# Scattering token rows from SBUF to expert slots, in a mixture-of-experts encoder layer

## The reference, cut to what matters

```
g_idx  = argmax of 4 group logits;  top-2 of the 8 experts in that group
w_pair = softmax(top_v) * g_w                     # two weights a token
dest   = slot of each (token, expert) pair, experts padded to blocks
xbuf   = x_pad[slot_tok]                          # rows by slot
out    = (silu(xb @ w_gate[e]) * (xb @ w_up[e])) @ w_down[e]
y      = sum over a token's two slots of w_pair * out
x      = LN(alpha * x + (1 + gate) * y)
```

## Time and profile before

| | |
|---|---|
| median of 3 runs | 1818.4 us (1818.11, 1818.4, 1822.61) |
| profiled execution | 1822.78 us |
| its span | 1820.8 us, mean granted clock 0.923 |
| PE busy | 1549.7 us (85%) |
| DVE, ACT, POOL busy | 610.3, 331.0, 112.4 us |
| moved by DMA | 298.91 MB |

### The profile page before, as it was taken

One profiled execution on the slowest core, in us unless ns is written; L12 is line 12 of the kernel. 1 busy time (PEld: TensorE's weight loads), 2 busy tenths in 40 slices (PEclk: granted clock), 3 DMA queues, 4 the chain that ended last, 5 costly groups with the idle time before them and its releaser, 6 DMA issues. The chain is left out here.

```text
span 1820.8 us, 21099 instructions
## 1 busy us (share of the span) xinstructions
PE 1549.7 (85%) x7448; PEld 864.4 (47%) x7449; DVE 610.3 (34%) x1045; ACT 331.0 (18%) x566; POOL 112.4 (6%) x110
## 2 busy tenths in 40 slices
PE   5999999868875889999899543899999999999948
PEld 1455544336761766666455341444444444444423
DVE  1222144536886333333576640111111111101007
ACT  1101122212223333333211100101010101011111
POOL 0000000000002000000000032111111111101100
PEclk7999999977896899999999756999999999999979
DMA  9101011050006020000311106988889889999937
GB/s 365 56 23 35 1 12 46 12 185 1 0 0 225 15 93 0 0 0 0 136 65 63 48 0 197 365 319 293 319 332 381 322 319 396 392 333 393 395 133 297
DMA packets 145973, 298.91 MB, mean 164 GB/s; under 512 B 25596, under 2 KB 35848, under 8 KB 144915
## 3 DMA queue, kind: packets, MB, share of 16 engines
q1 hardware_dynamic: 137412, 280.73, 42.0%
q0 software_dynamic: 8384, 16.81, 2.6%
q10 hardware_dynamic: 146, 0.98, 0.2%
HBM read 282.85 MB, written 25.73 MB: 169 GB/s over the span
## 5 line engine op out<-in xcount | busy, mean ns | idle before, releaser
L382 PE MATMUL ps<-w_in_tok,uT_tiles 128*128 128x512 f32 (+2 forms) x512 | 191.5, 535 | 1.2 <-ACT uT_tiles L303 1.2
L1799 PE MATMUL ps<-w_gate_sb,x_slotsT 128*128 x320 | 145.3, 608 | 9.9 <-issue 7.5
L1828 PE MATMUL ps<-w_down_sb,hidT 128*128 x320 | 142.1, 597 | 11.1 <-DVE hidT L1885 11.1
L1799 PE MATMUL ps<-w_up_sb,x_slotsT 128*128 x320 | 140.6, 592 | 0.0
L382 PEld LDWEIGHTS ps<-w_in_tok,uT_tiles 128*128 128x128 f32 x512 | 97.7, 192 | 89.8 <-issue 61.2
L1398 PE MATMUL ps<-w_out,hT 128*128 128x512 f32 x256 | 114.5, 601 | 0.0
L1880 DVE TENSOR_TENSOR hid<-silu_g,ps 128x512 f32<-128x512 f32 x20 | 13.8, 688 | 294.1 <-PE ps L1799 294.1
L463 PE MATMUL ps<-uT,mod 128*128 128x512 f32 x256 | 110.1, 592 | 1.7 <-ACTq L470 1.7
L1799 PEld LDWEIGHTS ps<-w_gate_sb,x_slotsT 128*128 128x128 f32 x320 | 60.2, 193 | 87.7 <-issue 87.7
L1799 PEld LDWEIGHTS ps<-w_up_sb,x_slotsT 128*128 128x128 f32 x320 | 60.8, 190 | 76.5 <-issue 76.5
L1828 PEld LDWEIGHTS ps<-w_down_sb,hidT 128*128 128x128 f32 x320 | 59.1, 190 | 79.7 <-issue 79.7
(11 more groups left out here) (372 smaller groups left out, 2026.8 us busy)
## 6 DMA issues: line engine op xcount, KB each, us to landing
light_gate_sb<-in_w_gate SPq DMA_DIRECT2D x20, 2048.0 KB, 13.2
light_up_sb<-in_w_up SPq DMA_DIRECT2D x20, 2048.0 KB, 19.4
light_down_sb<-in_w_down SPq DMA_DIRECT2D x20, 2048.0 KB, 13.6
w_gate_sb<-in_w_gate SPq DMA_DIRECT2D x12, 2048.0 KB, 9.8
w_up_sb<-in_w_up SPq DMA_DIRECT2D x12, 2048.0 KB, 15.2
w_down_sb<-in_w_down SPq DMA_DIRECT2D x12, 2048.0 KB, 20.1
uT<-in_w_ada SPq DMA_DIRECT2D x8, 2048.0 KB, 9.9
y_pair<-expert_rows SPq DMA_DIRECT2D x8, 1024.0 KB, 10.7
```

The source lines that it names most:

```text
L382: mm = nc.tensor.matmul(ps[:, 2 + g, 0:n], uTt[:, j, k, :], wt[:, k, c0:c0 + n], start=k == 0, stop=k == KD - 1)
L1799: m = m_.matmul(ps[:, bank, :], xT[:, k, :], wt[:, bass.ds(buf, 1), k, :].rearrange("p a f -> p (a f)"), start=k == 0, stop=k == KD - 1)
L1828: m = m_.matmul(ps[:, 5 + half, :], hT[:, k, :], wd[:, bass.ds(buf, 1), k, half * 512:half * 512 + 512].rearrange("p a f -> p (a f)"), sta ...
```

## The change

The u2 rows now stay in SBUF. A tensor `big` (128 x 8 x 1024) lives for the whole kernel and is in turn uT, the keys and values of attention, u2, and the light gate and up weights.

- mLSTM stage: POOL zeroes `gate2`, and SP writes it over all 7680 slot rows of a DRAM tensor `xslots` in six DMAs; the stage ends when they have landed.
- Attention stage: behind `w_out`, SP copies `xslots` to `yslots` from DRAM to DRAM in six DMAs, awaited at the end of the output projection.
- Output projection: no store of u2; the router bias is loaded here.
- Routing: two products over all 256 columns give per-tile counts and ranks inside a tile; DVE sums the counts and adds them up tile by tile. The block table is made across 128 partitions, one block number a partition, and turned to one row by five small products. The pair weights are formed later. The map, its scatters and reads are gone.
- Experts: POOL first scatters the u2 rows to their slots (16 indirect DMAs of 128 rows), waits for all, and only then adds the increment that lets SP load light weights. A block's x is then a plain load of its slots, and y a plain store (five DMAs, the light block in four quarters).
- Combine: POOL gathers each tile's two y rows by slot.

```diff
@@ mlstm
+            def _(pool):
+                nc.gpsimd.memset(self.gate2[:], 0.0).then_inc(s_zero, 1)
...
+                n = NSLOT // P // 6
+                sp.wait_ge(s_zero, 1)
+                for i in range(6):
+                    sp.dma_start(rows[:, i * n:(i + 1) * n, :], self.gate2[:].unsqueeze(1).to_broadcast([P, n, D])).then_inc(s_cleared, 16)
+                sp.wait_ge(s_cleared, 16 * 6)
@@ attend
                 sp.dma_start(self.wo[:], self.i["w_out"].rearrange("(k p) n -> p k n", p=P)).then_inc(self.s_wo, 16)
+                n = NSLOT // 6
+                for i in range(6):
+                    sp.dma_start(self.yslots[i * n:(i + 1) * n, :], self.xslots[i * n:(i + 1) * n, :]).then_inc(self.s_yzero, 16)
@@ output_projection
+                sp.dma_start(self.br[:, 0:NG], self.i["b_rg"].partition_broadcast(P)).then_inc(s_br, 16)
+                sp.dma_start(self.br[:, NG:], self.i["b_re"].partition_broadcast(P)).then_inc(s_br, 16)
...
-                    sp.wait_ge(s_u, t + 1)
-                    sp.dma_start(u2_t[t], u2[:, t % 2, :]).then_inc(s_st[t % 2], 16)
+                sp.wait_ge(self.s_yzero, 16 * 6)
@@ routing
-                for t in range(TT):
-                    for j in range(t + 1):
-                        m = nc.tensor.matmul(ps[:, 0, t * E:(t + 1) * E], self.c(C_ONE if j < t else C_US), A[:, j, :], start=j == 0, stop=j == t)
-                for j in range(TT):
-                    m = nc.tensor.matmul(ps[:, 1, 0:E], self.c(C_ONE), A[:, j, :], start=j == 0, stop=j == TT - 1)
-                m.then_inc(s_rank, 1)
+                nc.tensor.matmul(ps[:, 1, 0:TT * E], self.c(C_ONE), Af, start=True, stop=True)
+                nc.tensor.matmul(ps[:, 0, 0:TT * E], self.c(C_US), Af, start=True, stop=True).then_inc(s_rank, 1)
+                pe.wait_ge(s_cols, 1)
+                for j in range(5):
+                    m = nc.tensor.matmul(ps[:, 2, j * NB:(j + 1) * NB], col[:, j:j + 1].to_broadcast([P, P]), self.c(C_ID, NB), start=True, stop=True)
+                m.then_inc(s_rows, 1)
...
+                lk(v.tensor_reduce(cnt[:], ps[:, 1, 0:TT * E].rearrange("p (t e) -> p e t", e=E), AX, ALU.add))
...
+                for t in range(TT - 1):
+                    lk(v.tensor_tensor(base[:, t + 1], base[:, t], ps[:, 1, t * E:(t + 1) * E], ALU.add))
...
+                lk(v.tensor_scalar(cmp_[:, 0], bend[:], pcol, None, ALU.is_le))
+                lk(v.tensor_scalar(cmp_[:, 1], lend[:], pcol, None, ALU.is_le))
...
+                lk(v.tensor_reduce(col[:], cmp_[:], AX, ALU.add))
+                v.tensor_scalar_min(col[:, 0:2], col[:, 0:2], float(E - 1)).then_inc(s_cols, 1)
...
+                for at, j in ((0, 0), (6, 1), (1, 2), (3, 3), (2, 4)):
+                    lk(v.tensor_copy(self.tbl[:, at], row(j)))
@@ experts
+                def load(b):
+                    g.dma_start(xg[:], self.xslots[b * P:(b + 1) * P, :]).then_inc(s_xg, 16)
...
+                def store(b):
                     pool.wait_ge(s_yd, b + 2)
+                    g.dma_start(self.yslots[b * P:(b + 1) * P, :], ys[:]).then_inc(s_out, 16)
                     pool.wait_ge(s_lyd, b + 2)
+                    rows = self.yslots[LB + b * LC:LB + (b + 1) * LC, :]
+                    for q in range(4):
+                        g.dma_start(rows[:, q * Q:(q + 1) * Q], yl[q * LC:(q + 1) * LC, :]).then_inc(s_lout, 16)
...
+                for k in range(2):
+                    for t in range(TT):
+                        g.indirect_dma_start(out=self.xslots, out_offset=bass.IndirectOffsetOnAxis(ap=self.posi[:, k, t:t + 1], axis=0),
+                                             in_=self.big[:, t, :], in_offset=None).then_inc(s_x0, 16)
+                pool.wait_ge(s_x0, 16 * 2 * TT)
+                pool.sem_inc(s_lG, 1)
+                load(0)
+                load_light(0)
@@ combine
+            def _(pool):
+                for t in range(TT):
+                    if t >= B:
+                        pool.wait_ge(s_sum, t - B + 1)
+                    for k in range(2):
+                        nc.gpsimd.indirect_dma_start(out=yt[:, t % B, k, :], out_offset=None, in_=self.yslots,
+                                                     in_offset=bass.IndirectOffsetOnAxis(ap=self.posi[:, k, t:t + 1], axis=0)).then_inc(s_y[t % B], 16)
```

More of the change, by code:

```diff
@@ L45 @@
 C_IOTA = C_INV + 32
-C_END = C_IOTA + NB
+C_PCOL = C_IOTA + NB
+C_END = C_PCOL + 1
 def constants():
@@ L67, in constants @@
     c[:, C_IOTA:C_IOTA + NB] = np.arange(NB)
+    c[:, C_PCOL] = np.arange(P)
     return c
@@ L732, in mlstm, with _ @@
             chunk = lambda i, d: i if d == 0 else i * -1 + (TT - 1)
+            @block.gpsimd
+            def _(pool):
+                nc.gpsimd.memset(self.gate2[:], 0.0).then_inc(s_zero, 1)
+            @block.sync
+            def _(sp):
+                rows = self.xslots.rearrange("(r p) d -> p r d", p=P)
+                n = NSLOT // P // 6
[3 more added lines that the diff above has]
+                sp.wait_ge(s_cleared, 16 * 6)
             @block.scalar
@@ L1282, in output_projection @@
             "varA", "stdA", "varB", "stdB", "u2_ready", "u2_turned", "u2T_ready", "logits_product", "logits_copied"))
-        s_st = [self.sem(f"u2_stored{j}") for j in range(2)]
+        s_br = self.sem("b_router_loaded")
         s_x1, s_x1st = self.sem("x1_ready"), self.sem("x1_stored")
@@ L1315, in _ @@
                     sp.dma_start(x1_t[t], x1[:, t, :]).then_inc(s_x1st, 16)
-                    sp.wait_ge(s_u, t + 1)
-                    sp.dma_start(u2_t[t], u2[:, t % 2, :]).then_inc(s_st[t % 2], 16)
-                for j in range(2):
-                    sp.wait_ge(s_st[j], 16 * TT // 2)
+                sp.wait_ge(s_br, 32)
+                sp.wait_ge(self.s_yzero, 16 * 6)
                 sp.wait_ge(s_x1st, 16 * TT)
@@ L1511, in routing @@
             hv, lt, lend = sb("is_heavy", [P, E]), sb("is_light", [P, E]), sb("light_end", [P, E])
[L1512 removed]
+            hst, prev = sb("heavy_start", [P, E]), sb("start_ahead", [P, E + 1])
+            base = sb("slot_base", [P, TT, E])
             pos = sb("pos", [P, 2, TT])
[L1514 to L1544 removed]
+            cmp_ = sb("cmp", [P, 5, E])
+            col = sb("table_cols", [P, 5])
             @block.scalar
@@ L1646, in _ @@
[L1646 to L1653 removed]
+                lk(v.tensor_copy(self.posi[:], pos[:]))
@@ new lines, in _ @@
+                dve.wait_ge(s_e2, 1)
+                lk(v.tensor_scalar_add(sel[:], eg[:], 1.0))
+                lk(v.reciprocal(sel[:], sel[:]))
+                lk(v.tensor_tensor(self.wts[:, 0], sel[:], gw[:], ALU.mult))
+                lk(v.tensor_tensor(self.wts[:, 1], eg[:], self.wts[:, 0], ALU.mult))
+                dve.wait_ge(s_rows, 1)
+                row = lambda j: ps[0:1, 2, j * NB:(j + 1) * NB]
+                for at, j in ((0, 0), (6, 1), (1, 2), (3, 3), (2, 4)):
+                    lk(v.tensor_copy(self.tbl[:, at], row(j)))
@@ L1656, in experts @@
+                lk(v.tensor_scalar_mul(self.tbl[:, 5], row(2), 16.0))
+                lk(v.tensor_tensor(self.tbl[:, 4, 0:1], bend[0:1, E - 1:E], lend[0:1, E - 1:E], ALU.max))
     def experts(self):
@@ L1757, in _ @@
                         pool.wait_ge(s_xt, b + 1)
-                        gather(ahead)
+                        load(ahead)
                         pool.wait_ge(s_lxt, b + 1)
-                        gather_light(ahead)
+                        load_light(ahead)
                     if b > 0:
                         with pool.If(n > b - 1):
-                            scatter(b - 1)
+                            store(b - 1)
             @block.tensor
@@ L1780, in _ @@
                 n = count(pe)
-                for s in (s_G, s_U, s_Y, s_ht, s_lG, s_lY, s_lht):
+                for s in (s_G, s_U, s_Y, s_ht, s_lY, s_lht):
                     pe.sem_inc(s, 1)
```

175 lines of the change are left out of this document (50 added, 125 removed).

## The result

The changed kernel took 1828.11 us (median of 13 runs, 1823.0 to 1835.2). The kernel before, run beside it, took 1822.15 us (13 runs, 1818.11 to 1826.91). The ratio is 1.0037, with a 95% interval of 1.002 to 1.0053: slower, by a little more than what can be told from no change. The forecast was 1802.0 with a range of 1786 to 1822. The profiled execution took 1830.28 us, its span 1828.4, at a mean granted clock of 0.923; the span is 7.6 us longer than before, where the forecast had 16.4 less.

The account below looks back on a forecast made before the run. Routing was taken as latency-bound, the experts as PE with DMA right behind, the combine as PE. Terms -15.2 - 6.7 + 3 + 2 + 0.5 = -16.4 us on the 1818.4 median gave 1802.0 us, range 1786 to 1822.

Parts of the forecast that it names:

- start of routing: Routing's front: the earlier bias load saves 3.6 us, moving the exponential's wait and its two followers away saves 0.8 us.
- ranks: Routing: 44 small rank products become two with 256 columns, 19.1 us falling to 2.3, so -16.8 us.
- slots ready: Routing: the point at which DVE has the slots, forecast at 1053.8 against 1072.98 before.
- first scatter to the last landed: Before the experts: 16 POOL scatters share DMA bandwidth with heavy weights, starting at 1061.6 and all landed by 1099.
- first x load: Before the first expert product: 4.7 us from issue to landing, plus 0.3, landed at 1104.0.
- first product: First expert product starts at 1108.1 instead of 1123.25, -15.2 us.
- first block: First expert block: light weights land before their use, removing the wait for light_up and the slow clock after it, -6.7 us.
- later blocks: Experts: whole blocks loaded and stored add DMA traffic, so late weight waits grow, +3 us, between 0 and 8.
- tail: End of the experts: three more POOL stores and engines walking through unused iterations, +2 us, between 0 and 5.
- combine: Combine: pair loads move to POOL and only the first pair may be late, +0.5 us, between 0 and 2.
- clearing and copying: mLSTM and attention stages: clearing and copying slot rows hide beside idle DMA, 0 us.
- the one of no change: Rival: scatters end at 1103, x load takes twice 4.7 us, waits, tail and combine grow; about +2, 1820 us; chance 0.09.

Follow-up runs that it names:

- e2: The changed kernel, with the light weights of block 0 let go only after the first x rows have landed; median 1824.89 us, 1.0011 of before.
- e3: The changed kernel, with x1 tiles 1 to 3 of the combine issued only after the first y pair has landed; median 1827.78 us, 1.0024 of before.
- e12: The changed kernel, with only x1 tiles 2 and 3 of the combine behind the first y pair; median 1820.34 us, 0.9994 of before.
- e8: The changed kernel without the stores of y rows, so its output lacks the experts' part; 1818.48 us in one profiled run.
- e9: The kernel before, with all expert loops bounded by the number of blocks and POOL's skips grouped; median 1818.69 us, 0.9984 of before.
- e4: The kernel before, with only the ranks by two wide products and DVE's sums over tiles; median 1807.57 us, 0.9915 of before.
- e6: The changed kernel, with 37 never-executed products put ahead of PE's expert loop; median 1824.11 us, 1.0009 of before.
- e10: The kernel before, with the wide rank products, the earlier router bias and expert loops bounded by the number of blocks; median 1802.99 us, 0.988 of before.
- e5: The changed kernel, with expert loops of SP, PE, ACT and DVE bounded by the number of blocks, POOL's skips grouped; median 1813.01 us, 0.995 of before.
- e11: The changed kernel, with bounded expert loops, light weights after the first x, and x1 tiles 2 and 3 behind the first y pair; 1800.47 us, 0.9882 of before.

## Why the prediction was wrong

By its own steps, from the profiled executions:

| step | forecast, us | measured, us |
|---|---|---|
| start of routing | -3.6 - 0.8 | -2.9 - 0.85 |
| ranks | -16.8 | -16.9 |
| sums of the counts | +2.0 | +2.0 |
| slots ready | 1053.8 | 1054.29 |
| end of routing to first scatter | 1.6 | 2.2 |
| first scatter to the last landed | 37.4 | 40.3 |
| first x load | 5.0 | 9.1 |
| x landed to first product | 4.1 | 4.7 |
| first product | -15.2 | -6.1 |
| first block | -6.7 | -7.1 |
| later blocks | +3 (0 to 8) | +6.9 |
| tail | +2 (0 to 5) | +6.15 |
| combine | +0.5 (0 to 2) | +7.7 |
| clearing and copying | 0 | 0 |
| sum | -16.4 | +7.6 |

The -2.9 is a difference of two points in time; by DVE's wait the earlier bias is worth 3.5. The sum missed by 24.0 us: 9.1 in the first product, 7.2 in the combine, 4.2 in the tail, 3.9 in the later blocks, and 0.4 the other way in the first block. On the medians the miss is 26.1, as the 1802.0 stood on 1818.4, the median of 3 runs of before, and that of 13 is 1822.15. The changed kernel lies outside the range without this too: 1.0037 times 1818.4 is 1825.

**Right**: the ranks, the slots, the table, the first block (28.07 us from the first product to the next light load before, 20.97 after) and the copy. Two passes at 404 GB/s had been the dearer bound for the copy; it moved 31.46 MB at 327 GB/s with the DMA engines at a share of 1.00, and the last part landed 105 us after its issue, behind w_out, long before 877.85. By the Trainium skill (DMA: Bandwidth & Descriptors, Latency and other measured facts) copies of tiles between HBM tensors reached 207 to 214 GB/s at best, in a layout with rows far apart. The 327 GB/s of this contiguous copy do not agree, and the measurement decides.

**The step that failed first is "Then the x load, 4.7 us from issue to landing".** That row was taken where the DMA engines had little else to do. The change itself frees 6.3 MB of light weights in the instant in which it issues this load, and the prediction said so in its next paragraph ("frees SP for the light weights at 1099") without bringing the two together. It measured 9.1 us, and 3.9 once the weights wait (e2). Of the 9.1 us by which the first product missed its forecast, 4.1 are this, 2.9 the scatters (taken at 1099, where the bound at 360 GB/s said 1103, which it was), 1.5 the later first scatter, 0.6 what follows the load.

**The tail, "+2", between 0 and 5,** was argued from POOL's issues, and POOL had never been last. The words "I cannot see whose walk ends last" gave up too early: the rows of the stage's line show it (PE, 0.96 us for each of 28 empty iterations). The mechanism, the same loop at a slower pace in another place of the program, was in no rival.

**The combine, "+0.5", between 0 and 2,** took "some 4 us" from issue to landing for the first pair, out of no row. It stands behind four x1 tiles issued in the same moment, landed 11.3 us after POOL's first issue where the forecast had 6.5, and was 4.92 us late (with one tile ahead it was not late, e3; with two by 1.26, e12), and its products then ran 2.8 us longer than before. Together these are the 7.7. About 2 of them are peculiar to this execution, as the six kernels with the same combine show; that leaves 5.6. Two tiles ahead take 2.6 off (e12), and the other 3.0 are what e12 still has: 1.26 of wait and 1.7 of slower products.

**Later blocks, "+3", between 0 and 8:** the mechanism was right (e8), the size was not. The 9.2 us of waits stand against 4.6 of before, and 2.3 us more of PE's time go with them (564.64 us busy against 562.40 in the same blocks).

Of the rivals, the one of no change, where the bounds fall together, was nearest. Its conditions came about one by one: scatters at 1103, the x load at twice 4.7, the late waits near 8. It gave +2 on the span where +7.6 was measured, and of the difference 5.7 lie in the combine. It had 9 chances in 100, and its parts were not as independent as that: all but the tail are one fact, that the change fills the DMA engines just where loads that PE waits for are issued. The range ended at that rival's 1820 and a little above, so with the combine and the tail beyond their bounds (7.7 against 2, 6.15 against 5) and the base too low the range missed.

What stays open: why PE's empty iteration takes 0.74 or 0.96 us (one padding shows that the place matters, and the rows show between which two instructions), what sets the length of POOL's DRAIN, why e12 gained more by its ratio than by its stages, and why e9 gained 2.9 us by its ratio where its stages are 6.5 shorter, at the edge of its interval.

## What to carry to other kernels

Price a transfer by a row in which the queues are as full as they will be, and ask for each load on the path what the change issues in the same instant; a small load behind megabytes that nobody needs yet is mended by one wait (e2: 5.4 us of the stage). Split a change before judging it: here one edit was worth 0.85%, and the rest of it cost more. When a stage ends late, read each engine's last instruction on the stage's own line before naming who is late, and let hardware loops run as often as there is work.

## What the runs showed of the hardware that was not expected

- The same loop head on PE's sequencer came round every 0.74 us in before, e4 and e6, and every 0.96 us in after and the six kernels made from it that keep its 48 iterations without the padding; 37 products that are never executed, put ahead of it, brought the 0.74 back.
- POOL's DRAIN at the end of the stage took 6.8 us where indirect DMAs had carried the y rows (before, e9, e10), and 1.5 to 1.6 us where plain ones had (after, e5, e6, e11). Without any store it took 4.8 us (e8), so the kind of DMA alone does not explain it; the cause is open.
- A wait of PE of 4 to 5 us costs more than itself: the 64 light products behind 4.29 us took 6.36 us at a granted clock of 0.56, those behind 4.88 us 4.93 at 0.73, against 3.66 at 1.00; the pair's eight behind 4.92 us took 6.73 at 0.53, against 3.60 for the next pair's at 1.00.
- A plain DMA issued by POOL took 0.57 us of it, not the 1.27 of an indirect one with its gap. The landings of the DMAs that were new, from the page's part on DMA issues (KB each, median us from issue to landing):

```profile
slot_x_rows<-gate SPq DMA_DIRECT2D x6, 5120.0 KB, 38.4
...
x_slots<-slot_x_rows POOLq DMA_DIRECT2D x21, 512.0 KB, 6.7
...
slot_x_rows<-uT_kv_u_light,slot_of_pair POOLq DMA_INDIRECT x16, 13.2
y_pair<-slot_y_rows,slot_of_pair POOLq DMA_INDIRECT x16, 8.5
slot_y_rows<-slot_x_rows SPq DMA_DIRECT2D x6, 68.1
```
